# A bias row stored once per head and read in reverse, and a dt projection with its weights held and its result turned back

## The reference, cut to what matters

```python
zxbcdt = u @ in_proj                                   # (256, 2048) @ (2048, IN_DIM)
dt_raw = zxbcdt[..., D_INNER + CONV_DIM:]              # the last 64 columns, one per head
dt = jax.nn.softplus(dt_raw + dt_bias)
...
dist = qpos[:, None] - kpos[None, :]
bias = jnp.transpose(rel_bias[t5_causal_bucket(dist)], (2, 0, 1))
logits = logits + bias[None, :, None]
logits = jnp.where((dist >= 0)[None, None, None], logits, -jnp.inf)
```

## Time and profile before

| | |
|---|---|
| Time, three runs | 2656.53, 2654.6 and 2654.67 us, median 2654.67 us |
| The profiled execution | span 2654.2 us from first to last instruction; the page gives no other time for it, and the quickest run is 0.4 us longer |
| PE busy, PEld busy | 2578.9 us (97%), 2338.9 us (88%) |
| DVE, ACT, POOL busy | 1805.5 us (68%), 1203.1 us (45%), 138.4 us (5%) |
| DMA | 477.17 MB, mean 180 GB/s |
| Chain that ended last | PE 92%, DVE 4%, ACT 2%, DMA 1% |

### The profile page before, as it was taken

How to read it: one execution, slowest core, us unless ns; L and a number is a source line. 1 busy time by engine, 2 the same in 40 slices (tenths; PEclk the granted TensorE clock), 3 DMA queues, 4 the chain that set the end, 5 groups by cost and what they waited for, 6 DMA issues and landing times.

```text
span 2654.2 us, 44813 instructions
## 1 busy us (share of the span) xinstructions
PE 2578.9 (97%) x16616; PEld 2338.9 (88%) x16616; DVE 1805.5 (68%) x2617; ACT 1203.1 (45%) x1589; POOL 138.4 (5%) x261
## 2 busy tenths in 40 slices
PE   6999999999999999999999899999899999999997
PEld 6889988998889898989898888988689999999996
DVE  3777777776876656565656867767876666666666
ACT  3555445544554434343434644444453434343433
POOL 2220222012100000000000000000000000000000
PEclk8999999999999999999999999999999999999999
DMA  8665566556446666566666555555356665666664
GB/s 182 199 189 176 172 192 196 166 181 190 160 141 193 190 190 190 190 190 189 190 189 191 175 167 166 158 175 167 120 169 196 185 194 186 193 186 194 187 193 135
DMA packets 267175, 477.17 MB, mean 180 GB/s; under 512 B 16577, under 2 KB 50210, under 8 KB 265298
## 3 DMA queue, kind: packets, MB, share of 16 engines
q1 hardware_dynamic: 263296, 457.76, 55.7%
q0 software_dynamic: 3296, 18.12, 2.8%
q10 hardware_dynamic: 498, 0.18, 0.0%
HBM read 470.70 MB, written 5.31 MB: 179 GB/s over the span
## 4 chain that ended last, share of the span: by engine, by line
PE 92%; DVE 4%; ACT 2%; issue 1%; DMA 1%; POOL 0%; ACTq 0%; DVEq 0%; POOLq 0%; SPq 0%
PE ps L1241 29%; PE ps L1242 29%; PE ps L1243 29%; PE ps L1387 1%; ACT whl L562 1%; DVE whl L820 1%; ACT junk L565 1%; PE ps L1406 0%; DVE h L929 0%; DVE xhl L890 0%; DMA par_rows<-a_conv_b 0%; PE ps L1466 0%; DVE stat L842 0%; PE ps L1380 0%; PE ps L1390 0%
## 5 line engine op out<-in xcount | busy, mean ns | idle before, releaser
L820 DVE TENSOR_TENSOR whl<-raw,whl 128x1024 fp32r<-128x1024 f32 x865 | 1069.8, 1237 | 771.3 <-ACT whl L562 761.9
L562 ACT ACTIVATE whl<-raw 128x1024 fp32r<-128x1024 f32 x865 | 916.2, 1059 | 1280.6 <-PE ps L1243 1253.9
L1241 PE MATMUL ps<-xhl,whl 128*128 128x256 f32 x3072 | 866.0, 282 | 6.3 <-DVE xhl L890 6.3
L1242 PE MATMUL ps<-xhl,whl 128*128 128x256 f32 x3072 | 859.2, 280 | 0.0
L1243 PE MATMUL ps<-xhl,whl 128*128 128x256 f32 x3072 | 858.7, 280 | 0.0
L1241 PEld LDWEIGHTS ps<-xhl,whl 128*128 128x128 f32 x3072 | 580.1, 189 | 11.4 <-DVE xhl L890 7.7
L1242 PEld LDWEIGHTS ps<-xhl,whl 128*128 128x128 f32 x3072 | 580.2, 189 | 2.9 <-issue 1.7
L1243 PEld LDWEIGHTS ps<-xhl,whl 128*128 128x128 f32 x3072 | 580.0, 189 | 0.0
L1241 PE MATMUL ps<-whl,bhl 128*128 128x512 f32 x1408 | 552.0, 392 | 4.7 <-DVE bhl L951 3.6
L1242 PE MATMUL ps<-whl,bhl 128*128 128x512 f32 x1408 | 550.5, 391 | 0.0
L1243 PE MATMUL ps<-whl,bhl 128*128 128x512 f32 x1408 | 549.9, 391 | 0.0
(11 more groups left out here) (194 smaller groups left out, 1877.6 us busy)
## 6 DMA issues: line engine op xcount, KB each, us to landing
raw<-mlp_w SPq DMA_DIRECT2D x512, 512.0 KB, 4.1
raw<-a_in_proj SPq DMA_DIRECT2D x161, 512.0 KB, 4.5
raw<-a_out_proj SPq DMA_DIRECT2D x64, 512.0 KB, 4.5
raw<-b_w_q SPq DMA_DIRECT2D x32, 512.0 KB, 3.7
raw<-w_k SPq DMA_DIRECT2D x32, 512.0 KB, 3.7
raw<-w_v SPq DMA_DIRECT2D x32, 512.0 KB, 3.7
raw<-b_out_proj SPq DMA_DIRECT2D x32, 512.0 KB, 3.7
cumb<-cum_scratch POOLq DMA_DIRECT2D x8, 1024.0 KB, 7.7
```

The costliest lines, as they stand in the source:

```text
L562: sc.activation(whi[:, s.split, :], raw[:, s.raw, :], ACT.Copy).then_inc(hi_ready, 1)
L820: ve.tensor_tensor(out=wlo[:, s.split, :], in0=raw[:, s.raw, :], in1=whi[:, s.split, :].bitcast(F32), op=ALU.subtract).then_inc(lo_ready, 1)
L1241: te.matmul(outs, lh, rh, start=start, stop=False, skip_group_check=True)
L1242: te.matmul(outs, lh, rl, start=False, stop=False, skip_group_check=True)
```

## The change

The bias row is kept in DRAM once per head (24 KB in place of 3 MB) and its order is turned round: the masked stretch first, then distance rising from left to right. A table load now lets partition p start one element further than partition p - 1 in the same row, and DVE reads the table backwards (`[::-1]`).

The dt projection is `head_major` in place of `token_major`: the 64 dt columns are the weights, all 256 tokens pass by, 16 x 3 = 48 matmuls, and the result has heads on partitions. DVE copies it from PSUM to `cumt` (a tile that is free until the running sums are turned), and PE turns it back with two transposes (`turn_dt`), which stand in PE's order behind step xs 0. DVE waits for them (`dt_done`) before it goes on with dt as before.

```diff
-        bias_dram = nc.dram_tensor("bias_scratch", [HEADS, P, S + P], F32, kind="Internal").ap()
+        bias_dram = nc.dram_tensor("bias_scratch", [HEADS, P + S], F32, kind="Internal").ap()
...
-            g_.memset(bias_row[:, S:S + P], MASKED)
+            g_.memset(bias_row[:, 0:P], MASKED)
             for b in range(BUCKETS):
-                lo, hi = S - bounds[b + 1], S - bounds[b]
+                lo, hi = P + bounds[b], P + bounds[b + 1]
...
-            pool.dma_start(bias_dram, bias_row[:, :].unsqueeze(1).to_broadcast([HEADS, P, S + P])).then_inc(bias_out, 16)
+            pool.dma_start(bias_dram, bias_row[:, :]).then_inc(bias_out, 16)
...
-                src = bass.AP(tensor=bias_dram.tensor, offset=g * (HG * P * (S + P)) + P - 1,
-                              ap=[[S + P - 1, P], [P * (S + P), HG], [1, S]])
+                src = bass.AP(tensor=bias_dram.tensor, offset=g * (HG * (P + S)) + 1,
+                              ap=[[1, P], [P + S, HG], [1, S]])
...
             dve.wait_ge(slab_used, mix.slab(0).used)
+            ve.tensor_copy(cumt[:, :], ps[0:NH, 7, 0:S]).then_inc(dt_rows, 1)
+            dve.wait_ge(dt_done, 1)
...
-                        for t, cols, bias in ((1, slice(0, S), tab[:, i, :]), (0, slice(S, S + P), tab[:, i, P:])):
+                        for t, cols, bias in ((1, slice(0, S), tab[:, i, ::-1]), (0, slice(S, S + P), tab[:, i, P - 1::-1])):
...
+            def head_major(s):
+                pe.wait_ge(lo_ready, s.n + 1)
+                wh, wl = slot(s, KT)
+                for k in range(KT):
+                    last = three(ps[0:NH, 7, 0:S], (wh[:, k, :], wl[:, k, :]), (xhi[:, k, :], xlo[:, k, :]),
+                                 start=k == 0, stop=k == KT - 1)
+                last.then_inc(slab_used, 1)
+
+            def turn_dt():
+                pe.wait_ge(dt_rows, 1)
+                for c in range(MT):
+                    last = te.transpose(ps[:, 7, c * NH:(c + 1) * NH], cumt[:, c * P:(c + 1) * P], ident[0:NH, 0:NH])
+                last.then_inc(dt_done, 1)
...
-            token_major(mix.slab(0), 0, 1, 7, x, tiles=16, cols=NH)
+            head_major(mix.slab(0))
...
+                if first and (unit, i) == ("xs", 0):
+                    turn_dt()
```

More of the change, by code:

```diff
@@ L324, in build @@
         dve_chain, act_chain, pool_chain = sem("dve_chain"), sem("act_chain"), sem("pool_chain")
+        dt_rows = sem("dt_rows")
         dt_done, dt_v, dt_e, dt_l, da_ready, cum_done, cum_ready = (
```

## The result

| | before | after |
|---|---|---|
| Median time | 2655.41 us (2654.6 to 2656.53, 4 runs) | 2638.17 us (2636.09 to 2640.45, 4 runs) |
| Ratio | | 0.9935, 95% interval 0.9922 to 0.9949 |
| Profiled span | 2654.2 us | 2635.5 us (the same execution took 2637.44 us) |

The kernel is 17.2 us faster, where 12.3 us were forecast, and 2638.17 us lies 0.8 us under the range. So the sign is right, the size is 3 to 5 us short, and on which side of the range's end a median falls is partly luck.

The account below looks back on a forecast made before the run. PE, busy for 97% of the span, was taken as the bound. Starting xs 4 at 51.45 instead of 63.76 us saves 12.3 us: 2654.7 - 12.3 = 2642.4 us, range 2639.0 to 2645.8 us.

Parts of the forecast that it names:

- the start: From the dt projection to PE's step xs 4: xs 4 at about 51.45 instead of 63.76 us, saving 12.3 us.
- The projection and the clock: dt projection on PE: 48 matmuls, clock low for 3.4 us from 33.5 us, 1.5 us lost, end at 38.6 us.
- the rows at 108 us: Profile rows used as model for the clock: 2.5 us idle, wide matmuls, fall 1.1 us later lasting 3.4 us.
- The slab: Input slab 4, without the 3 MB write: lands at 30 to 37 us, hidden until ACT splits it at 38.9 us.
- the slab is still late: Rival, chance 0.05: slab 4 lands at 51 us as before, PE idles in the turn, gain nil, 2654.7 to about 2656 us.
- The turn back and slab 5: After xs 0: PE waits 0.2 us, dt begins at 42.1 us, slab 5 ready at 51.4 us, xs 4 at 51.45 us.
- The table: Bias table loads and DVE's reversed reads: both cost nothing; loads have 47 us before first use, reads as long as forward.
- everything behind is released by PE or by this chain, so I see nothing that gives the gain back: Program behind xs 4: slabs follow at 1.24 us each against PE's 2.8 us, so the 12.3 us saved stays.

Follow-up runs that it names:

- after_again: The changed kernel run and profiled once more with no edit; 2640.41 us, ratio 0.9936 to the kernel before.
- after_pad: The changed kernel with one more unused small DVE copy before the first step of dt; 2639.68 us, ratio 0.9939 to the kernel before.
- dt_only: The changed kernel with the bias part undone (128 copies in DRAM, forward reads), new dt projection kept; 2653.18 us, ratio 0.9988 to the kernel before.
- the two pairs of profiles: Kernel before and changed kernel, each profiled twice without edit; medians 2655.41 and 2638.17 us first, 2656.65 and 2640.41 us second.
- before_pad_late: The kernel before with one unused one-column DVE copy behind the attention's last steps; 2655.52 us, ratio 0.9996 to the kernel before.
- before_pad: The kernel before with one unused DVE copy of PSUM where the changed kernel has its copy; 2653.03 us, ratio 0.9987 to the kernel before.
- before_fill: The kernel before with 24 unused wide matmuls in PE's idle time before the dt projection; 2654.08 us, ratio 0.9993 to the kernel before.

## Why the prediction was right about the start and wrong about the sum

- **The projection and the clock.** 38.6 us were forecast for its end with a fall, from a start at 31.48 us: 7.1 us. It took 7.26 us. The fall came and lasted 3.4 us, as the rows at 108 us had it (where the idle time is 2.3 us, not 2.5 us); with the gap filled it did not come and about 1.5 us were won back. That the fall was just as long as forecast is luck: in after_again, and in after_pad, whose start is the same up to dt, it lasted 6.8 us and the projection 8.2 to 8.3 us. The Trainium skill's sentence ("TensorE: Matmul & The Clock Gate", Part 1) that the clock is throttled by default and released by activity agrees with the fall behind the idle gap. The kernel before shows something else: there the clock stayed at 0.50 for 16.7 us in which PE was never idle.
- **The slab.** It is hidden behind the projection, as forecast. If the 3 MB write stays, the slab can be split only at 50.69 us and the clock falls while PE waits, which costs all the gain of the start. This was the rival "the slab is still late", and dt_only is its price.
- **The turn back and slab 5.** The wait for the turn, dt at 41.43 us (forecast 42.1, from a start 0.65 us later) and xs 4 at 50.82 us (forecast 51.45) are each within 0.1 us of the forecast, counted from PE's start, in the first profile. In the second, dt begins at 43.82 us and xs 4 at 53.21 us, both about 1 us later counted so, with the longer fall.
- **The table.** Reads and loads were put at nothing, and that was right.
- **The step that failed** is "everything behind is released by PE or by this chain, so I see nothing that gives the gain back". It looked for losses and put what the rest of the program gives at nothing. But the program behind the start did not keep its length: the copy of the turn back is one more instruction in DVE's order, and with it DVE's stall between the passes of the attention's loop is 2.5 to 2.7 us in place of 4.8 us or more. That is worth 4.0 and 4.1 us in the two pairs of profiles, about half of it the stall and half the clock's fall behind it, and 2.3 us where the clock does not fall (before_pad_late); in whole runs one instruction gave 3.0 us (before_pad, 1.1 to 5.8 us by its interval). 12.3 + 4.0 = 16.3 us lies between the 15.7 and 17.2 us measured, but the sum is rough: in the spans of the first pair the earlier start of PE adds 0.65 us and the way from xs 4 to the attention 2.5 us, and 0.7 us is lost at the end; in the second pair these are -0.2, 0.4 and -1.4 us, and the start gives 14.2 us. Before_pad gives a check: with the short stall in both, the start is worth about 2653.03 - 2639.2 = 13.8 us, where 2639.2 us is the median of all nine runs of the changed kernel. So the start is 12.3 to 14.2 us; it was sized from one profile of a kernel whose projection took 18.7 us there and 20.5 us in the next.
- **Two smaller ones.** The range was drawn from three runs 1.9 us apart; the kernel before spreads over 6 us in the 27 runs timed beside the first experiments (2653.32 to 2659.4). And between span and time there are 1.9 us, not 0.5 us.

That the place of DVE's instructions sets the stall is shown by before_pad and before_pad_late. By which means stays open: the profile's waits name no releaser ("issue") or one that was long done, and the packets of q14 point to the loading of DVE's instructions without proving it.

## What to carry to other kernels

Where a projection has few columns, try holding those as weights and letting the tokens pass by. Here that made half as many matmuls, and a clock that was low for 3.4 to 6.8 us and not to the end of the projection. Look then at what the slow stretch was hiding: here a broadcast write of 3 MB, which was free before and would have cost the start's whole gain after. And when a measured gain differs from a well-founded sum by a few microseconds, lay the two traces beside each other along the whole program: a stall that moves with one instruction is no merit of the change, and an unused instruction can show it. Take more than one profile of each kernel first: the stages that agree between the pairs are the effect, and the others are what differs from run to run.

## What was not expected of the hardware

- A single DVE instruction ahead of a loop moved a stall between the loop's passes: 4.8 to 5.1 us in five profiles of four kernels with the old order, 2.3 to 2.7 us with one instruction more, 3.2 us with two. Two packets of an instruction queue, of 8 KB each, lie at this jump back and at no other one of DVE.
- TensorE's granted clock fell to 0.50 with PE busy without a break, 3.6 us into a stream of 64-column matmuls (before_fill), and stayed there for the remaining 13.5 us of it.
- An operand read backwards cost DVE nothing: 479 ns (128x256) and 343 ns (128x128) against 480 and 343 ns. The Trainium skill ("Vector Engine (DVE) Microarchitecture Reference", 5.1) lists an operand with a negative step among what is not measured; for this fp32 form it now is.
